# Projections of a two-layer trunk with weights as the stationary operand, and GpSimd's first convolution weights copied ahead of its residual scaling

## What is computed

```python
# layer 0: sliding-window attention, 32 query heads, 4 key/value heads, sinks, relative bias
qkv = x @ w_qkv
# layer 1: forgetting attention, 32 heads, logits carry a cumulated decay
proj = x @ w_qkvf                      # q, k, v of 2048 columns each, and 32 columns of decay
def conv_ffn(x, w_up, conv_w, conv_b, w_down):
    h = x @ w_up                       # 2048 -> 2 * 5632
    h = causal depthwise convolution of width 3 over tokens, plus conv_b
    g, u = h[..., :D_FF], h[..., D_FF:]
    return (jax.nn.silu(g) * u) @ w_down
x = layer_norm(ALPHA * x + y, ln_g[i, s], ln_b[i, s])     # after each mixer and each MLP
```

## Time and profile before

| what | value |
|---|---|
| median of 3 runs | 2332.55 us (2331.82 to 2332.85) |
| the profiled execution | 2332.9 us, its span 2331.2 us |
| PE busy | 2274.6 us, 98% of the span |
| PEld busy | 1818.0 us, 78% |
| DVE, ACT, POOL busy | 1368.9, 1072.7, 210.5 us |
| DMA | 408.47 MB, 175 GB/s over the span |

### The profile page before, as it was taken

One profiled execution on the slowest core, in us unless ns is written; L12 is line 12 of the kernel. 1 busy time (PEld: TensorE's weight loads), 2 busy tenths in 40 slices (PEclk: granted clock), 3 DMA queues, 4 the chain that ended last, 5 costly groups with the idle time before them and its releaser, 6 DMA issues.

```text
span 2331.2 us, 31747 instructions
## 1 busy us (share of the span) xinstructions
PE 2274.6 (98%) x10331; PEld 1818.0 (78%) x10331; DVE 1368.9 (59%) x1856; ACT 1072.7 (46%) x1431; POOL 210.5 (9%) x216
## 2 busy tenths in 40 slices
PE   9999989999999999999999999989999999999996
PEld 7777868888888878887777877877888888878885
DVE  4555576666566654447664554675566656664445
ACT  4444445555555543335444444354555555543332
POOL 2000040000000000003420120031000000000001
PEclk9999999999999999999999999999999999999998
DMA  8434546665666555565654654555656565665553
GB/s 255 134 125 159 191 129 190 180 180 180 180 180 180 181 183 187 188 188 155 207 162 133 199 167 138 175 158 175 186 174 186 175 185 176 184 214 187 187 187 108
DMA packets 206936, 408.47 MB, mean 175 GB/s; under 512 B 12652, under 2 KB 13756, under 8 KB 206620
## 3 DMA queue, kind: packets, MB, share of 16 engines
q1 hardware_dynamic: 200192, 385.92, 53.9%
q0 software_dynamic: 5776, 21.34, 3.2%
q10 hardware_dynamic: 908, 0.43, 0.1%
HBM read 405.46 MB, written 2.18 MB: 175 GB/s over the span
## 4 chain that ended last, share of the span: by engine, by line
PE 92%; DVE 3%; POOL 2%; DMA 2%; ACT 0%; issue 0%; SPq 0%; ACTq 0%; DVEq 0%; POOLq 0%
PE ps L1171 28%; PE ps L1172 28%; PE ps L1173 28%; PE ps L1250 2%; DMA lnp<-in_ln_b_dram 2%; PE ps L1274 1%; PE ps L1267 1%; POOL res L401 1%; PE ps L1266 1%; POOL res L398 1%; PE ps L1287 1%; PE ps L1288 1%; PE ps L1286 0%; DMA raw<-in_a_w_qkv_dram 0%; PE ps L1295 0%
## 5 line engine op out<-in xcount | busy, mean ns | idle before, releaser
L760 DVE TENSOR_TENSOR w_lo<-raw,w_hi 128x1024 fp32r<-128x1024 f32 x728 | 904.5, 1253 | 490.2 <-ACT w_hi L480 489.6
L480 ACT ACTIVATE w_hi<-raw 128x1024 fp32r<-128x1024 f32 x728 | 770.6, 1059 | 866.5 <-PE ps L1173 827.3
L1171 PE MATMUL ps<-w_lo,xh 128*128 128x512 f32 x1952 | 789.8, 405 | 26.5 <-DVE w_lo L760 11.7
L1172 PE MATMUL ps<-w_hi,xl 128*128 128x512 f32 x1952 | 774.3, 397 | 0.0
L1173 PE MATMUL ps<-w_hi,xh 128*128 128x512 f32 x1952 | 774.3, 397 | 0.0
L1171 PEld LDWEIGHTS ps<-w_lo,xh 128*128 128x128 f32 x1952 | 368.5, 189 | 121.4 <-DVE w_lo L760 12.0
L1173 PEld LDWEIGHTS ps<-w_hi,xh 128*128 128x128 f32 x1952 | 368.2, 189 | 89.0
L1172 PEld LDWEIGHTS ps<-w_hi,xl 128*128 128x128 f32 x1952 | 368.9, 189 | 81.3
L1171 PE MATMUL ps<-w_lo,hid_h 128*128 128x512 f32 x704 | 278.6, 396 | 0.0
L1173 PE MATMUL ps<-w_hi,hid_h 128*128 128x512 f32 x704 | 278.4, 396 | 0.0
L1172 PE MATMUL ps<-w_hi,hid_l 128*128 128x512 f32 x704 | 278.4, 396 | 0.0
(11 more groups left out here) (155 smaller groups left out, 1451.1 us busy)
## 6 DMA issues: line engine op xcount, KB each, us to landing
raw<-in_ffn_w_up_dram SPq DMA_DIRECT2D x352, 512.0 KB, 3.7
raw<-in_ffn_w_down_dram SPq DMA_DIRECT2D x176, 512.0 KB, 4.6
raw<-in_b_w_qkvf_dram SPq DMA_DIRECT2D x96, 512.0 KB, 4.2
raw<-in_a_w_qkv_dram SPq DMA_DIRECT2D x40, 512.0 KB, 3.8
raw<-in_a_w_o_dram SPq DMA_DIRECT2D x32, 512.0 KB, 4.3
raw<-in_b_w_o_dram SPq DMA_DIRECT2D x32, 512.0 KB, 4.6
bias<-rel_by_distance POOLq DMA_DIRECT2D x4, 1024.0 KB, 6.6
bias<-minus_cumulated_decay POOLq DMA_DIRECT2D x4, 1024.0 KB, 5.9
```

Source lines behind the costliest of these rows:

```text
L480: act.activation(w_hi[:, loc % RING], raw[:, loc % RING], ACT.Copy).then_inc(high_ready, 1)
L760: dve.tensor_tensor(w_lo[:, s], raw[:, s], w_hi[:, s].bitcast(FP32), ALU.subtract).then_inc(low_ready, 1)
L1171: pe.matmul(o, lh[:, k, rows], w_lo[:, slot, k % 2, :], start=(k == 0), stop=False)
L1172: pe.matmul(o, ll[:, k, rows], w_hi[:, slot, k % 2, :], start=False, stop=False)
```

## The change

Q of layer 0, Q and K of layer 1 and the gate and up projections now use `turned_product`: a 128x128 block of the weight is the stationary operand, and the 256 tokens of `xh` or `xl` stream past it. For one k tile there are four such blocks by three matmuls: twelve matmuls of 256 columns in place of six of 512. The result stands in PSUM already turned, so `tok_copy` and `turn_tok` go for these groups. K of layer 0 keeps them. The Q groups of layer 0 now alternate between the two bank sets, and their loops are written out. ACT's convolution stands at slots 1 and 3 in place of 3 and 5, DVE's at 3 and 5 in place of 5 and 7. On POOL the copies for the first pair of each MLP stand ahead of `scale_residual`.

```diff
+            def turned_product(s, turn, k, slot):
+
+                for j in range(4):
+                    if k == 0 and j % 2 == 0:
+                        pe.wait_ge(acc_free[s][j // 2], turn)
+                    cols = slice(j * P, (j + 1) * P)
+                    o = ps[:, 2 * s + j // 2, (j % 2) * SEQ:(j % 2 + 1) * SEQ]
+                    pe.matmul(o, w_lo[:, slot, k % 2, cols], xh[:, k, :], start=(k == 0 and j % 2 == 0), stop=False,
+                              skip_group_check=True)
+                    pe.matmul(o, w_hi[:, slot, k % 2, cols], xl[:, k, :], start=False, stop=False, skip_group_check=True)
+                    last = pe.matmul(o, w_hi[:, slot, k % 2, cols], xh[:, k, :], start=False, stop=(k == KT - 1),
+                                     skip_group_check=True)
+                return last
...
                 def turn(n, b4, first=False):
-                    for k in group(0, n * 2 + t0, b4, 0, before=x_ready(1 + 2 * l) if first else None, tile0=tok_tile0):
+                    for k in turned_group(0, n + t0, b4, 0, before=x_ready(1 + 2 * l) if first else None):
                         if first:
                             x_next(1 + 2 * l, k)
-                        elif k == 2:
-                            turn_tok(1, n * 2 + (t1 - 1), 1, n * 2 + (t1 - 1))
-                    for k in group(1, n * 2 + t1, b4, KC, tile0=tok_tile0):
-                        if k == 2:
-                            turn_tok(0, n * 2 + (t0 + 1), 0, n * 2 + (t0 + 1))
+                    for k in turned_group(1, n + t1, b4, KC):
+                        pass
...
-                last_turn = t1 + 2 * UP_PAIRS - 1
-                turn_tok(1, last_turn, 1, last_turn)
...
-                with pe.Fori(0, GROUPS - 1) as i:
-                    for k in group(1, i + (TURN_A_Q + 1), i * (KC // 4) + (CH_A_Q + KC) // 4, 0, tile0=tok_tile0):
-                        woven(k, i + 1)
+                for n in range(1, GROUPS):
+                    for k in turned_group((n + 1) % 2, TURN_A_Q[(n + 1) % 2] + n // 2, (CH_A_Q + n * KC) // 4, 0):
+                        woven(k, n)
...
+            def first_conv_weights(l):
+                for h in range(2):
+                    wait_free(gp, h, TURN_UP[l][h])
+                    gp.tensor_copy(cw[:, h], convcol[:, l, :, h * FT:h * FT + 4]).then_inc(cw_ready, 1)
+
             def conv_weights(l):
-                with gp.Fori(0, UP_PAIRS) as n:
+                with gp.Fori(1, UP_PAIRS) as n:
...
+            gp.wait_ge(par_ready, 5)
+            first_conv_weights(0)
             gp_loads = scale_residual(0, 0, 0, gp_loads)
-            gp.wait_ge(par_ready, 5)
             conv_weights(0)
...
+            first_conv_weights(1)
             gp_loads = scale_residual(1, 0, 2, gp_loads)
             conv_weights(1)
```

More of the change, by code:

```diff
@@ L528, in xt_evacuate, with q_copy, turned_copy @@
                 act.activation(xh[:, 2 * g:2 * g + 2, :], src, ACT.Copy).then_inc(xt_high, 1)
[L530 to L544, removed]
+            def q_copy(s):
+                act.activation(qT[:, 0:2, :].rearrange("p a (m t) -> p (a m) t", t=P), backwards(bank(s, 0)), ACT.Copy, scale=SCALE)\
+                   .then_inc(acc_free[s][0], 1)
+            def turned_copy(dst, s, scale=1.0):
+                act.activation(dst[:, 0:2, :], bank(s, 0).rearrange("p (a t) -> p a t", a=2), ACT.Copy, scale=scale)\
+                   .then_inc(acc_free[s][0], 1)
             def attend(s, hc, sink):
@@ L688, in turn @@
                 def turn(n, b4, first=False):
-                    if not first:
-                        up_copy(l, n - 1)
                     for k in slots(b4, 0):
@@ L998, in turn @@
                             out_residual(0, 0)
-                with dve.Fori(0, GROUPS - 1) as i:
-                    own.enter(i, 4)
-                    turn(i + 1, i * (KC // 4) + (CH_A_Q + KC) // 4)
-                    own.leave(GROUPS - 1)
+                for n in range(1, GROUPS):
+                    turn(n, (CH_A_Q + n * KC) // 4)
                 turn(GROUPS, CH_O[0] // 4, 2 * KT)
@@ L1176, in product, with turned_group @@
                 return last
+            def turned_product(s, turn, k, slot):
[10 more added lines that the diff above has]
+                return last
+            def turned_group(s, turn, b4, loc0, before=None):
+                for k in range(KT):
+                    loc = loc0 + k // 2
+                    if k % 2 == 0:
+                        if before:
+                            before(k // 2)
+                        pe.wait_ge(low_ready, b4 * 4 + (loc + 1))
+                    last = turned_product(s, turn, k, loc % RING)
+                    if k % 2 == 1:
+                        last.then_inc(chunks_used, 1)
+                    yield k
             def group(s, turn, b4, loc0, lh=xh, ll=xl, nk=KT, before=None, tile0=None):
@@ L1323, in mixer_a @@
             def mixer_a():
-                for k in group(0, TURN_A_KV, CH_A_KV // 4, 0, before=x_ready(0), tile0=tok_tile0):
+                for k in group(0, TURN_A_KV, CH_A_KV // 4, 0, before=x_ready(0)):
                     x_next(0, k)
-                for k in group(1, TURN_A_Q, CH_A_Q // 4, 0, tile0=tok_tile0):
+                for k in turned_group(1, TURN_A_Q[1], CH_A_Q // 4, 0):
                     if k == 1:
@@ L1362, in first_waits @@
                     def first_waits():
-                        wait_free(pe, 1, n * 2 + t1)
-                        wait_free(pe, 0, n * 3 - 1 + t0)
+                        wait_free(pe, 1, n + t1)
+                        wait_free(pe, 0, n * 2 - 1 + t0)
                     attention_slot(k, (n + (GROUPS - 1)) * HG, (n + (GROUPS - 1)) * 2, False, first_waits,
-                                   lambda: wait_free(pe, 0, n * 3 + t0))
+                                   lambda: wait_free(pe, 0, n * 2 + t0))
                 def turn(n, b4, first=False):
-                    for k in group(0, n * 3 + t0, b4, 0, before=x_ready(2) if first else None, tile0=tok_tile0):
+                    for k in turned_group(0, n * 2 + t0, b4, 0, before=x_ready(2) if first else None):
                         if first:
```

129 lines of the change are left out of this document (52 added, 77 removed).

## The result

| | before | after |
|---|---|---|
| median of 4 runs | 2332.26 us (2331.82 to 2332.85) | 2264.03 us (2263.54 to 2264.11) |
| span of the profiled execution | 2331.2 us | 2261.4 us |

The ratio is 0.9707 (95% interval 0.969 to 0.9724): the changed kernel is 68.2 us faster by the medians. I had said 2238.2 us. The forecast's sign and range hold, its size is 26 us off, and the time is 3 us from the second rival's 2267.

The account below looks back on a forecast made before the run. The prediction took PE, busy 98% of the span, to bound the kernel. Its terms summed as 2332.9 - 28.7 - 48.7 - 15.4 - 3.4 + 1.5 = 2238.2 us, with a range from 2226 to 2378.

Parts of the forecast that it names:

- second rival: In the turned groups, streams cost by the column whatever their number, 116.7 ns per matmul: 2267 us; chance 0.08.
- term 1: Turned groups: 5376 matmuls of 512 columns become 10752 of 256 at 114 ns each, -28.7 us.
- p: Spacing on PE of a 256-column matmul with a 128-column load behind it, taken as 114 ns.
- single pair: Last decay matmul with a 128-column load behind it: 110 to 120 ns, read as load and stream not waiting.
- the prediction's own sign: In MLP groups: wrong if the 256-column spacing passes 116 ns, or every group shows bank-set or `w_lo` waits on PE.
- likeliest case: Turned groups' streams at 112 to 116 ns, with or without POOL's gain: 2225 to 2268 us, chance 0.52.
- first rival: Every 128-column load costs PE its 20 ns, at all 10752 matmuls: 2374 us, slower; chance 0.32.
- term 2: 56 of 57 turns go from PE's program, 0.87 us each: -48.7 us.
- term 3: First pair of each MLP: POOL's `cw` copies ahead of the residual end PE's idle and half clock, -15.4 us.
- third rival: Behind a norm, POOL's order frees nothing because DVE starves PE all the same: 2253 us; no separate chance given.
- term 4: Waits of the turned path, between up and down projection and in three Q groups, go: -3.4 us.
- term 5: Given back: layer 1's first K group waits longer for DVE's decay chain, first groups after norms are activation-paced; +1.5 us.

Follow-up runs that it names:

- Experiment 1: Changed kernel plus ten rows of 48 extra float32r matmuls behind its work, varying moving columns, loaded columns and data; 256 columns with 128 loaded took 116.7 ns.
- experiment 12: Changed kernel with only `oh`, `ol`, `hid_h` and `hid_l` moved by pads to the weight ring's place modulo 64; 2245.34 us.
- experiment 6: Changed kernel plus twelve rows of 48 matmuls behind its work, varying loaded tile, moving tile and PSUM bank; 113.3 to 120.0 ns for 256 columns.
- experiment 4: experiment 2 with the MLP's convolution, SiLU, product and split put back to the slots of the kernel before, two later; 2281.83 us.
- experiment 5: Kernel before with each 512-column product matmul cut into two of 256, the same stationary tokens loaded again for each; 2370.72 us.
- the grid: Changed kernel plus 34 rows of 24 matmuls of 256 columns, mainly six moving-tile offsets by five stationary-tile offsets; only spacings count.
- experiment 7: Changed kernel plus 28 rows of 24 matmuls of 256 columns, operands fixed in each row, varying offsets, tiles and loaded widths; only spacings count.
- experiment 10: Changed kernel with `xh` and `xl` lying 4 elements past the weights' place modulo 64 instead of 8; 2271.28 us.
- experiment 2: Changed kernel with POOL's first two copies of convolution weights put back behind the residual scaling; 2286.59 us, ratio 0.981.

## Why the prediction was right in its sign and 26 us off

**The streams (term 1) were mis-sized: -28.7 us forecast, 0 measured.** The step that failed is "From these I take p = 114 ns: a stream needs 113.6". The 113.6 came from the decay rows, and I read it as what 256 columns need, because I took the load's width for the only other thing that differed. Experiment 1 has the same 32-column load at 119.8 ns, so the width alone was not it. The place of `wf_hi` and `wf_lo` against `xh` and `xl` has a part: the pads of experiment 12 also move these two from place 40 to 32, and there the 48 decay matmuls take 5.52 / 47 = 117.4 ns each, where they take 113.3 to 114.2 in all eleven traces with both at their old places.

```profile
1066.02 0.28 PE L1374 MATMUL ps<-xh,wf_lo 128*32 128x256 f32 x1
...
1071.54 0.28 PE L1376 MATMUL ps<-xh,wf_hi 128*32 128x256 f32 x1
```

It is not all: blocks of 32 columns at the same two differences, 0 and 32 in turn, took 116.7 in experiment 6. The single pair in the earlier trace rows was one reading at a resolution of 10 ns and could not tell 114 from 117. Against the evidence of one unlike row stood the second rival's, 233.3 over thousands of matmuls, to which I gave 0.08 only. It happened exactly: 116.7 is half of 233.3. By the prediction's own sign ("I am wrong if p is above 116 ns") its account of the streams is wrong. Its range for the likeliest case, 2225 to 2268, was also narrower than its terms: 112 ns would give 2217, and 116 ns without POOL's gain 2275. That the measured time lies inside the range is in part luck: the other terms came out, 114 did not.

**The first rival's mechanism is refuted.** A load of 128 columns costs nothing more beside a stream of 256 than beside one of 512: experiment 1 has 116.7 ns for the first and 232.7 or 233.3 for the second with loads of 32 or 128. That the same 20 ns stand on 512 columns and 10 on 256 was the sign that it goes with columns.

**The turns (term 2) were right.** A group is 22.40 instead of 23.27 us, 0.87 less, and the one set of eight transposes that is left is K's in layer 0. In layer 1's mixer eight of them are the whole change: 6.96 forecast, 7.0 measured.

**POOL's order (term 3) was right**: -16.3 us alone for -15.4, and the wait of `cg` for `cw` stands in no row of the changed kernel's waits. The third rival, that it would free nothing, is refuted. Taken from the changed kernel the same order is worth 22.6; of the 6.3 more, some 4.8 come from the convolution's earlier slots (experiment 4), and 1.5 stay unassigned, which is less than the spread of these runs. The prediction had costed the slots at nothing, which holds only with the copies ahead; this was the cover that they hang on, and I had not priced it.

**The waits (term 4) were right as far as they can be seen**: layer 0's mixer gives 4.96 us for 4.7. Between up and down projection the 1.34 us of the earlier trace rows are one step of the stream (the timeline of PE after):

```profile
793.09 0.28 PE L1157 MATMUL ps<-xh,w_hi 128*128 128x256 f32 x1
793.21 0.40 PE L1140 MATMUL ps<-w_lo,hid_h 128*128 128x512 f32 x1
```

**Given back (term 5): +1.5 us forecast, about 0 measured.** PE comes to the decay chain's end earlier, but so does the chain, which is fed by PE's own decay matmuls. Its wait is 0.94 us where it was 0.97:

```profile
1101.24 0.31 PE L1380 MATMUL ps<-ident,fs 32*128 32x32 f32 x2 [0.94 <-DVE fs L1009]
```

Where PE's work shrinks, a wait grows only if what it waits for doesn't start from PE too.

In all: 2238.2 + 28.7 for the streams, and -2.9 for the small terms together (1.5 of it term 5), give 2264.0.

**What stays open.** Why the spacing depends on the two places as it does, what the width of the load has to do with it, why a stream of three alternating products goes at 113.3, 116.7 or 118.7 ns at the difference 4 where fixed blocks have 113.35, and what stopped PE in experiment 5's down projections.

## What to carry to other kernels

A rate over thousands of instructions of the kernel's own stream outweighs a better one read from a short row of another shape and other tiles; a rival that needs no new mechanism ("half the columns, half the time") deserves more than 0.08. Making operands turned by the choice of the stationary side cost PE nothing here and saved each turn and its waits. A wait that is hidden by another edit should be priced with that edit gone: here the convolution's earlier slots cost 4.8 us as soon as `cw` is late. Where matmuls bound a kernel, try where the stationary tile begins relative to the moving one, in the real stream and not on a fixed pair: 56 elements of padding gave 18.7 us.

## What the hardware showed that I had not expected

- The spacing of float32r matmuls with their loads depends on where the moving operand begins relative to the stationary one, modulo 64 elements (256 bytes): 113.35 to 122.5 ns for 256 columns, 227.15 to 233.35 for 512, with loads of 128 columns. Moving both by the same amount (but for one pair of the grid, 1.5 ns off), another PSUM bank, 64 partitions, or zeros as data change it by at most 0.3 ns.
- The place isn't all of it. For loads of 128 columns and fixed blocks the same difference gave the same spacing in each run (0: 120 ns in three of them). At the difference 0, loads of 96 and 64 columns gave 116.0 and 113.35. And one fixed block of 32 columns against `hid_h`'s first tile ran at 113.3 ns in experiment 6 and at 117.8 in experiment 7.
- A stream of the same tiles at the same places ran at 113.3 ns, then behind a wait of 0.7 us at 116.7, and in a later MLP of the same execution at 118.7 (experiment 10). The decay matmuls of experiment 2's trace begin at 116 to 120 ns and go over to 113.3 after nine. So a pace can also hang on what went before; no experiment here was made for that.
- A 512-column matmul takes 232.7 ns with a load of 32 columns, 231.0 with 64 and 233.3 with 128; one of 128 columns behind a load of 128 takes 110.6 ns.
- The clock fell to half for some 3 us after a norm in the kernel after too, where PE had waited 2.5 us and then run for 1.3 us: the steps are 0.21 us at 306 us in its timeline, and 0.12 again from 307.8; the granted clock from 304.5 to 306 is 0.50.
